# A hybrid gMLP/conformer layer with a 32-expert MoE on one core: expert weights without staging, merged rank and count products, earlier small loads

## The reference

```python
p = einsum('btd,dk->btk', rmsnorm(x, g), w_in)          # 1024 -> 6 * 1024
u_a, v_a, c_val, c_gate, g_a, g_b = split(p, 6)
v_a = layernorm(gelu(v_a)); u_a = gelu(u_a)
y_a = (u_a * chunk_spatial_mix(v_a, w_spatial)) @ w_branch_a
conv = depthwise_causal_conv31(c_val * sigmoid(c_gate))
y_b = silu(layernorm(conv)) @ w_branch_b
x = x + (sigmoid(g_a) * y_a + sigmoid(g_b) * y_b) @ w_out
# MoE on rmsnorm(x): 32 experts, 4 per token
logits = h @ w_router;  top 4;  gates = softmax(top 4 logits)
for each expert e and its tokens:
    gu = xb @ w_up[e] + b_up[e]                          # 1024 x 2048
    act = (clip(up) + 1) * min(gate, 7) * sigmoid(1.702 * gate)
    out = act @ w_down[e] + b_down[e]                    # 1024 x 1024
y = sum of gate * out per token;  final rmsnorm
```

## Time and profile before

| | |
|---|---|
| median of 3 runs | 1298.35 us (1297.46 to 1301.08) |
| the profiled execution's own time | 1300.47 us |
| its span in the trace | 1298.5 us |
| PE busy | 1182.5 us (91%) |
| DVE, ACT, POOL busy | 605.0, 249.5, 467.2 us |
| DMA traffic | 448.97 MB, mean 346 GB/s over the span |
| first up product of the MoE phase | starts at 341.02 us |
| last down product | starts at 1285.59 us |

### The profile page before, as it was taken

The page is one execution under the profiler, slowest core; times in us unless marked ns, Lnnn a source line. Parts: engine busy times, 40 slices in busy tenths (PEclk is TensorE's granted clock), DMA queues, the critical chain, the costliest instruction groups (busy, mean ns, idle before and its releaser), DMA issues.

```text
span 1298.5 us, 30625 instructions
## 1 busy us (share of the span) xinstructions
PE 1182.5 (91%) x11129; PEld 583.8 (45%) x11130; DVE 605.0 (47%) x1256; ACT 249.5 (19%) x487; POOL 467.2 (36%) x833
## 2 busy tenths in 40 slices
PE   8999999999999899899778998989989799899876
PEld 6777777775544233333233442333433233333232
DVE  2999984121444344444342444443534244344243
ACT  2012124001122122122121221221211122122112
POOL 1012300000444444435452445454544444535452
PEclk9999999999799999999999999999999999999997
DMA  9983433244699999999999699999999999999996
GB/s 260 339 260 106 142 118 134 100 142 184 244 391 390 422 421 420 422 421 421 421 421 421 252 405 420 422 421 421 422 420 421 421 421 422 421 421 422 421 421 253
DMA packets 94570, 448.97 MB, mean 346 GB/s; under 512 B 8526, under 2 KB 42894, under 8 KB 45339
## 3 DMA queue, kind: packets, MB, share of 16 engines
q1 hardware_dynamic: 93742, 446.55, 85.8%
q10 hardware_dynamic: 749, 1.19, 0.3%
q0 software_dynamic: 48, 0.85, 0.2%
HBM read 447.00 MB, written 2.42 MB: 346 GB/s over the span
## 4 chain that ended last, share of the span: by engine, by line
PE 55%; DMA 16%; DVE 12%; POOL 6%; issue 6%; SPq 4%; ACT 0%; DVEq 0%; POOLq 0%; ACTq 0%
PE banks L1371 20%; DMA ring<-in_w_down 15%; PE banks L1381 12%; DVE R L800 8%; PE banks L1164 8%; POOL ring L530 6%; PE banks L1086 4%; PE banks L1144 3%; PE banks L1123 3%; PE banks L1280 2%; PE banks L1130 1%; SPq L398 1%; DMA R<-in_conv_w 1%; PE banks L1153 1%; SPq L344 1%
## 5 line engine op out<-in xcount | busy, mean ns | idle before, releaser
L1371 PE MATMUL banks<-ring,hT 128*32 128x512 f32 x3328 | 431.6, 612 | 62.3 <-POOL ring L530 57.4
L530 POOL COPY ring<-big 128x512 f32<-128x512 f32 x248 | 146.9, 640 | 564.5 <-SPq L404 564.5
L530 POOL COPY ring<-R 128x512 f32<-128x512 f32 x496 | 289.8, 630 | 111.9 <-DMA R<-in_w_up 111.9
L321 DVE TENSOR_TENSOR xt<-xt,banks 128x1024 f32<-128x1024 f32 x106 | 128.7, 1215 | 401.2 <-PE banks L1144 401.2
L1381 PE MATMUL banks<-ring,hT 128*32 128x256 f32 x3328 | 226.2, 391 | 18.4 <-DMA ring<-in_w_down 13.1
L1381 PEld LDWEIGHTS banks<-ring,hT 128*32 128x32 f32 x3328 | 107.1, 113 | 201.1 <-issue 121.2
L1164 PE MATMUL banks<-hT,ring 128*128 128x288 f32 x768 | 192.0, 411 | 2.5 <-ACT R L602 2.2
L1371 PEld LDWEIGHTS banks<-ring,hT 128*32 128x32 f32 x3328 | 95.5, 111 | 197.5 <-POOL ring L530 81.7
L1164 PEld LDWEIGHTS banks<-hT,ring 128*128 128x128 f32 x768 | 147.2, 193 | 43.5 <-ACT R L602 2.6
L680 ACT COPY WT<-banks 128x256 f32<-128x256 f32 x52 | 19.4, 373 | 495.2 <-PE banks L1381 495.2
L800 DVE SCALAR_TENSOR_TENSOR R<-big,convw,R 128x256 f32<-128x256 f32 x240 | 108.1, 529 | 0.0
(11 more groups left out here) (254 smaller groups left out, 766.3 us busy)
## 6 DMA issues: line engine op xcount, KB each, us to landing
ring<-in_w_down SPq DMA_DIRECT2D x128, 1024.0 KB, 11.0
R<-in_w_up SPq DMA_DIRECT2D x124, 1024.0 KB, 18.1
ring<-in_w_up SPq DMA_DIRECT2D x70, 1024.0 KB, 9.4
big<-in_w_up SPq DMA_DIRECT2D x62, 1024.0 KB, 12.8
ring<-in_w_in SPq DMA_DIRECT2D x24, 1024.0 KB, 10.3
ring<-in_w_branch_b SPq DMA_DIRECT2D x4, 1024.0 KB, 5.0
ring<-in_w_branch_a SPq DMA_DIRECT2D x4, 1024.0 KB, 5.0
ring<-in_w_out SPq DMA_DIRECT2D x4, 1024.0 KB, 4.9
```

Source lines behind the costliest of these rows:

```text
L321: nc.vector.tensor_tensor(dst, dst, rows, ALU.add).then_inc(y_added, 1)
L530: ins = nc.gpsimd.tensor_copy(ring[:, k, h * 512:(h + 1) * 512], parked[k][:, h * 512:(h + 1) * 512])
L1371: ins = mm(UP[g * BLK:(g + 1) * BLK, :], xT[:, k, :], ring[:, k, g * 512:(g + 1) * 512], start=k == 0, stop=k == UP_SLOTS - 1)
```

## The change

Four edits, in the kernel's order:

- SP loads two weight blocks, then the small inputs (history, taps, `b_up`, spatial weights), then six blocks, instead of four, small inputs, four.
- The six parked buffers, the copies on GpSimd and the semaphores of both are gone. For each expert SP waits for each of the eight up slots to be used by the last item of the expert before, and loads it into the ring; then the same for the four down slots.
- ACT takes the square roots of the `v` layernorm between tiles 3 and 4 of its third group instead of 1 and 2.
- The ranks of the sample tokens and the counts over all rows come from one bank with shared products; the products over the prompt masks are issued ahead of the wait for the sample mask; one `keep_busy` call is gone, and the other four have two products of 256 columns instead of three of 32.

```diff
@@ SP, head of the program
-            for n in range(4):
+            for n in range(2):
                 load_block(n)
...
             load(cw_rows, a["conv_w"][0], cw_in)
             load(bup_rows, a["b_up"][0], bup_in)
             load(wsp, a["w_spatial"][0].rearrange("g i j -> i g j"), wsp_in)
-            for n in range(4, 8):
+            for n in range(2, 8):
                 load_block(n)
@@ SP, MoE phase
-            def load_parked(e, k):
...
-            def release_parked(before):
...
-            def load_up_rest(e, before):
-
-                for k in range(PARKED, UP_SLOTS):
+            def load_up(e, before):
+
+                for k in range(UP_SLOTS):
                     sp.wait_ge(up_used, before * UP_SLOTS + (k + 1))
                     load_slot(e, k)
...
-            sp.wait_ge(ya_evac, 2 * KC)
-            for k in range(PARKED - 1):
-                load_parked(1, k)
             for k in range(UP_SLOTS, SLOTS):
                 sp.wait_ge(*mix_block_used(MIX_BLOCKS - SLOTS + k))
                 load_slot(0, k)
-            load_parked(1, PARKED - 1)
             sp.wait_ge(before_known, 1)
-            with sp.Fori(1, NE - 1) as place:
+            with sp.Fori(1, NE) as place:
...
-                release_parked(before)
-                load_up_rest(here, before)
-                load_parked_again(place + 1, after, range(0, 2))
+                load_up(here, before)
                 load_down(here, before)
-                load_parked_again(place + 1, after, range(2, PARKED))
@@ POOL
-            for e in range(1, NE):
-                for k in range(PARKED):
-                    pool.wait_ge(parked_full[k], 16 * e)
-                    pool.wait_ge(released, (e - 1) * PARKED + k + 1)
-                    for h in range(4):
-                        ins = nc.gpsimd.tensor_copy(ring[:, k, h * 512:(h + 1) * 512], parked[k][:, h * 512:(h + 1) * 512])
-                    ins.then_inc(slot_full[k], 16)
@@ ACT
-                    if c == 2:
+                    if c == 4:
                         act.wait_ge(v_stats, 1)
@@ DVE
-            link(V.tensor_copy(rankm[:, 2, :], bank[5][:, NE:2 * NE]))
+            link(V.tensor_copy(rankm[:, 2, :], bank[4][:, NE:2 * NE]))
...
-            counts, count = DN[0:NE, 0:NE], DN[0:NE, NE:NE + 1]
+            counts, count = bank[4][0:NE, 2 * NE:3 * NE], DN[0:NE, 0:1]
@@ PE
-                    mm(TB[:, 0:NE], ones[:], below[:, 0:NE], start=True, stop=True)
+                    mm(TB[:, 0:256], ones[:], slot_ids[:, 0:256], start=True, stop=True)
...
-            for t2 in range(2):
-                mm(DN[:, 0:NE], ones[:], mask[:, t2, :], start=t2 == 0, stop=False)
-            mm(DN[:, 0:NE], ones[0:NS, :], mask[0:NS, 2, :], start=False, stop=True)
...
+            for t2 in range(2):
+                mm(bank[4][:, NE:3 * NE].rearrange("p (r e) -> p r e", r=2), ones[:],
+                   mask[:, t2:t2 + 1, :].to_broadcast([P, 2, NE]), start=t2 == 0, stop=False)
```

More of the change, by code:

```diff
@@ L54 @@
 DOWN_SLOTS = SLOTS - UP_SLOTS
-PARKED = 6
 MIX_BLOCKS = 36
@@ L211, in hybrid_layer @@
         slot_full = [sem(f"slot_full{k}") for k in range(SLOTS)]
-        released = sem("released")
-        parked_full = [sem(f"parked_full{k}") for k in range(PARKED)]
         vec_in, cw_in, cache_in, wsp_in, bup_in, lnv_in, wr_in = (
@@ L416, in load_down @@
                     load_slot(e, UP_SLOTS + j)
-            def load_parked_again(place, after, ks):
-                for k in ks:
-                    sp.wait_ge(slot_full[k], place * 16 + 16 * FILLS)
-                    load_parked(after, k)
             for k in range(UP_SLOTS):
@@ L1328, in _ @@
             sum_quarters(bank[0][:, 256:257])
-            keep_busy(3)
+            keep_busy(2)
             pe.wait_ge(h2T_ready, 5)
@@ L1340, in _ @@
             mm(bank[7][:, NE:2 * NE], below[:], mask[:, 1, :], start=False, stop=True).then_inc(rank_ready, 1)
-            keep_busy(2)
-            pe.wait_ge(routed, 3)
-            for t2 in range(2):
-                mm(bank[5][:, NE:2 * NE], ones[:], mask[:, t2, :], start=t2 == 0, stop=False)
-            mm(bank[5][:, NE:2 * NE], below_q[:].rearrange("p q t -> p (q t)"), mask[0:NS, 2, :], start=False, stop=False)
-            mm(bank[5][:, NE:2 * NE], same_row[0:NS].rearrange("p q t -> p (q t)"), rankm[0:NS, 2, :],
-               start=False, stop=True).then_inc(rank_ready, 1)
-            for t2 in range(2):
-                mm(DN[:, 0:NE], ones[:], mask[:, t2, :], start=t2 == 0, stop=False)
-            mm(DN[:, 0:NE], ones[0:NS, :], mask[0:NS, 2, :], start=False, stop=True)
-            for t2 in range(2):
-                mm(DN[0:NE, NE:NE + 1], mask[:, t2, :], ones[:, 0:1], start=t2 == 0, stop=False)
-            mm(DN[0:NE, NE:NE + 1], mask[0:NS, 2, :], ones[0:NS, 0:1], start=False, stop=True).then_inc(counted, 1)
+            for t2 in range(2):
+                mm(bank[4][:, NE:3 * NE].rearrange("p (r e) -> p r e", r=2), ones[:],
+                   mask[:, t2:t2 + 1, :].to_broadcast([P, 2, NE]), start=t2 == 0, stop=False)
+            for t2 in range(2):
+                mm(DN[0:NE, 0:1], mask[:, t2, :], ones[:, 0:1], start=t2 == 0, stop=False)
+            pe.wait_ge(routed, 3)
+            mm(bank[4][:, NE:2 * NE], below_q[:].rearrange("p q t -> p (q t)"), mask[0:NS, 2, :], start=False, stop=False)
+            mm(bank[4][:, NE:2 * NE], same_row[0:NS].rearrange("p q t -> p (q t)"), rankm[0:NS, 2, :],
+               start=False, stop=False)
+            mm(bank[4][:, 2 * NE:3 * NE], ones[0:NS, :], mask[0:NS, 2, :], start=False, stop=True).then_inc(rank_ready, 1)
+            mm(DN[0:NE, 0:1], mask[0:NS, 2, :], ones[0:NS, 0:1], start=False, stop=True).then_inc(counted, 1)
             for tt in range(2):
```

11 lines of the change are left out of this document (removed).

## The result

The changed kernel takes 1305.68 us (median of 6 runs, 1304.89 to 1308.54) against 1298.96 us (6 runs, 1297.46 to 1301.08): ratio 1.0056, 95% interval 1.0042 to 1.0069. It is 6.7 us slower. The forecast of 1304 us and its sign hold. The profiled execution of the changed kernel took 1305.68 us, its span is 1303.9 us; 1304.1 was predicted.

A forecast was written before the change was run, and what follows sets the result against it. The weight stream at 421 GB/s was taken to bound the MoE phase; first up product 7.0 us earlier, stream end at 1288.1, plus 16.0, gave a span of 1304.1, +5.6 us, so 1304 us; forecast 1301 to 1308, range 1297 to 1310.

The forecast's parts named there:

- Stream start: Start of the MoE loop: weight data flow 3.2 us after t0, the start of the first up product.
- The expert with three items: MoE phase: slots released one item later, so the stream stands still 14.6 us, and 1.7 in the expert behind.
- Pairs of two-item experts: MoE phase, one two-item expert after another: late release costs the stream 0.5 us each, 3 us at six pairs.
- Short queues and cold change-overs: MoE hand-overs between items: 1 us for short load queues, 2 us for change-overs at PE's lower clock.
- Standing still in all: MoE phase: the weight stream idles 22.6 us at late releases, plus 3 us of reserve for the hand-overs.
- GpSimd's copies: MoE phase: removing them gains 0, at most 3 us; they slow DVE where PE waits for data anyway.
- Roots: Square roots two tiles later: PE's 2.18 us wait and 1.8 us of lower clock go, -4.0 us, no new wait.
- Small inputs: Program start: loading them earlier removes PE's 1.28 us wait for the taps, -1.3 us; bounds +1.7 to -3.5.
- Routing: Rank and count products merged, `keep_busy` wider: -1.7 us from -1.1 to -2.9; 1 us more counted for item 0.
- The tail: End of the kernel: 16.0 us from the end of the weight stream to the end of the span.
- The rival that the front part pays for it all: Before and in item 0: PE stays at 2.4 GHz, cold change-overs cost nothing; 1297.5 to 1301 us, chance 0.30.
- The rival that every hand-over loses: MoE hand-overs: no 1.1 us room, from lower-clock change-overs or 2.0 us ahead of data; 1309 to 1315 us, chance 0.13.

The follow-up runs named there:

- e11_half_loads: The changed kernel with each load of an expert's slot bringing only the first half of its columns, all PE instructions kept: 1201.55 us.
- e9_late_head: The changed kernel with PE's two register reads of an item moved behind the gather products: 1292.96 us, ratio to before 0.9957.
- e7_inputs: The kernel before with only the small inputs issued two weight blocks earlier: 1298.10 us, ratio 0.9999.
- e4_routing: The kernel before with only the routing edit, merged rank and count products and 256-column `keep_busy` products: 1293.31 us, ratio 0.9959.
- e2_parked_kept: The changed kernel with the parked buffers, their loads and GpSimd's copies put back, the other three edits kept: 1288.55 us, ratio to before 0.9922.

## Why the prediction was right, and where not

The total was right to 0.2 us of span, more exactly than its terms were. Step by step:

- **The bound.** Right. The stream is it (`e11_half_loads`), at 421 GB/s with GpSimd's copies and without.
- **Stream start.** t0 + 3.2 predicted; flow at 335.05 against t0 = 332.18, 2.9. The first slot was done sooner than said (0.9 us, not 1.47) and SP's issue came later (0.36 us behind it, not 0.1).
- **Places 1 and 2.** 3.3 us predicted, 3.3 lost (335 to 402 us).
- **The expert with three items.** 14.6 predicted, 15.8 measured; the place behind it 1.7 and 1.8.
- **Pairs of two-item experts.** The step that failed: "needs 4.5 us for the change-over", taken from an item that had all its slots, and so "0.5 us, at six such pairs 3 us". Measured 1.6 at the first and 8.9 in the stretches that hold all (1.6 + 1.4 + 1.7 at 833 us + 4.2). PE's idle time at the head of the loop, where the register reads stand, is 0.24 us behind an item that had all its slots and 0.82 behind a paced one; the change-over is 5.1 us. SP's issue behind the release adds 0.3 (0.4 us where the prediction had 0.1). These 0.9 us, on top of the 0.5, make 1.4 of the 1.6 us. `e9_late_head` shows the larger part: 12.7 us come back for reads moved behind the gather. One of the prediction's own signs of being wrong, stream idle at two-item experts, came in part: at each of the pairs, not at each two-item expert.
- **Short queues and cold change-overs, 1 + 2 us.** Right in sum by luck. The change-overs behind paced items are not cold (1.07 us for eight products at 448.43). The reserve of 3 us covered half of the 5.9 that the pairs lost beyond their 3, by another mechanism.
- **Standing still in all.** 22.6 + 3 against 29.0: 3.4 us too few.
- **GpSimd's copies.** I took 0 off the path. No experiment has the copies without the buffers, so it isn't shown alone; but PE's idle time in the MoE phase went up, not down, though DVE lost its drag: its selections (L717, 128 x 32) take 237 ns on average against 411 beside the copies (median 235 against 240, longest 245 against 650: a few were held up long). The Trainium skill, "SBUF — State Buffer", "Who interferes with whom", with its exclusive port pair, agrees with that row, and the time shows that DVE was not on the path.
- **Roots, -4.0.** Measured -3.5 alone; 2.4 between the changed kernel's trace and before's. "I expect no new wait there" is wrong: 1.46 us of PE for DVE at 194.97. DVE's work from the statistics was next in line, as I had named it and then dismissed.
- **Small inputs, -1.3.** 0.0 alone (`e7_inputs`). I read one execution's wait as the kernel's: it is there when the program starts fast. The changed kernel's profile is of a slow start, and the 2.1 us that it is ahead at the first variance product aren't this edit's. In a fast start the prediction's bound of -3.5 had the right mechanism, the clock behind the transposes.
- **Routing, -1.7 and 1 for item 0.** -5.3 to -6.4 (`e4_routing`), beyond my bound of -2.9, and of -4.9 with the rival's 2 us for item 0: the clock stays high through the whole phase and through item 0. From the second block of logits (324.18 before, 319.76 after) to the first up product 16.8 became 12.4 us, and from there to the loop's first gather 11.8 became 9.5. Choosing the low clock as the nearest row was the error; the wide products were there to change just that.
- **The tail, 16.0.** 13.5. In before the last us of stream that I took as its end was followed by 2 us of a trickle; from the last slot's products to the end it is 12.9 and 12.7 us in the two, so nothing changed there, and my cut was in the wrong place.

In terms: t0 1.8 us earlier than said; the 1 us taken off the stream for item 0 came to 0.3; 3.4 more of standing still; 2.5 less behind it. That these errors come to -0.2 us is luck. The rival that the front part pays for it all was right on the front part (11.1 us by `e2_parked_kept`, where 10.4 and 2 for item 0 was its most); it fell because the parked buffers cost 15 to 17 us and not its 11.6. The rival that every hand-over loses had the right place and the wrong cause: paced change-overs were not at the lower clock (1.07 us at 448.43), and the data came 1.6 us behind the issue (333.45, 335.05), not 2.0.

## What to carry over

A double buffer isn't worth what it loads ahead of a loop but what it takes in while the consumer still holds its slots; ask at each hand-over when the slot comes free, not when its data could have come. Without such slack every fraction of a us between the last use of one item and the first of the next is on the stream's path: look there for instructions that no engine row shows, such as register reads at a loop's head, and put them behind queued work. And take a short wait at the program's start as a draw until a second profile shows it, and a gain ahead of a wait for another engine as nothing until that wait has gone.

## What was not expected of the hardware

- Register reads on PE's queue, two with their arithmetic: having them at the head of the loop and not behind the gather costs 0.44 us in each item that never waits, 0.99 us in one whose slots arrive one by one.
- The first projection products of the program take 406 or about 685 ns each with a granted clock of 1.00 in both cases; which of the two changes between executions, and it moved the transposes by 1.3 to 2.5 us. The Trainium skill, "TensorE: Matmul & The Clock Gate", part 1, says that the durations of the first matmuls differ between runs of one kernel; the rows agree, and the profile's clock column doesn't show it.
- One core's loads of weights run at 421 GB/s for 266 us and for 476 us on end. The Trainium skill, "DMA: Bandwidth & Descriptors", gives about 358 GB/s as a core's share when both cores of a pair stream; one streams here, and nothing here tests the other case.
- At half the bytes a slot, the core draws 230 GB/s on average, and PE still waits 1.8 to 4.1 us at ten places; ahead of the one looked at, busy DMA engines moved only 164 to 311 GB/s (`e11_half_loads`, 420 to 426 us). Why is open.
